# Two attention stages of one transformer layer pair on Trainium2: where a turned tile is rounded and its rest made in the second of them

## What is computed

```python
def moba_attention(q, k, v, rp_table):          # q, k, v: [B, T, H, dh], H = 8, dh = 64
    scale = dh ** -0.5
    ...
    s_own = jnp.einsum('hqd,hld->hql', qi, k_own) * scale + table_t[:, rel_bucket(d_own)]
    s_own = jnp.where(d_own[None] >= 0, s_own, -jnp.inf)
    ...
    p = jax.nn.softmax(s, axis=-1)
    return jnp.einsum('hqcl,hqcld->hqd', p_sel, v_sel) + jnp.einsum('hql,hld->hqd', p_own, v_own)

def second_block(x, mem, ...):
    h = rms_norm_2(x, norm_mix[l])
    qa, ka, va, qg, kg, vg, glr, rg = jnp.split(h @ w_in[l], offsets, axis=-1)
    o_a = moba_attention(qa, ka, va, rp_table)
    o_g = gla_chunked(qg, kg, vg, log_a)
    o_g = rms_norm_2(o_g, g_norm[l]) * jax.nn.silu(rg)
    x = x + jnp.concatenate([o_a, o_g], axis=-1) @ w_out[l]
    ...
```

## Time and profile before

| What | us |
|---|---|
| median of 3 runs | 1201.62 (1201.52 to 1201.82) |
| profiled execution | 1203.21, its span 1201.3 |
| busy: PE / DVE / ACT / POOL | 1185.0 / 741.9 / 622.9 / 146.2 |
| moba, 595 to 673 us: busy PE / DVE / ACT | 75.90 / 59.29 / 51.68 |
| fox, 60 to 140 us: busy PE / DVE / ACT | 80.00 / 49.79 / 48.54 |

### The profile page before, as it was taken

How to read it: one execution, slowest core, us unless ns; L and a number is a source line. 1 busy time by engine, 2 the same in 40 slices (tenths; PEclk the granted TensorE clock), 3 DMA queues, 4 the chain that set the end, 5 groups by cost and what they waited for, 6 DMA issues and landing times.

```text
span 1201.3 us, 16154 instructions
## 1 busy us (share of the span) xinstructions
PE 1185.0 (99%) x6066; PEld 988.1 (82%) x6066; DVE 741.9 (62%) x1124; ACT 622.9 (52%) x1054; POOL 146.2 (12%) x236
## 2 busy tenths in 40 slices
PE   9999999999999999999999999999999999999997
PEld 7788888678888888888788898888898888888886
DVE  6666567765333465674377775355647658559478
ACT  5556685675232345632676555352456355454464
POOL 3023123410000020000133100010001010000010
PEclk9999999999999999999999999999999999999999
DMA  6422234113443434342112445221286463753732
GB/s 197 106 53 54 71 105 106 36 53 105 105 105 105 158 112 137 105 127 71 50 54 105 158 125 160 85 88 53 89 245 140 149 150 88 217 116 87 211 71 88
DMA packets 151883, 133.35 MB, mean 111 GB/s; under 512 B 5313, under 2 KB 124161, under 8 KB 151810
## 3 DMA queue, kind: packets, MB, share of 16 engines
q1 hardware_dynamic: 144688, 113.13, 31.4%
q0 software_dynamic: 3744, 13.63, 5.9%
q10 hardware_dynamic: 3378, 5.60, 1.4%
HBM read 115.55 MB, written 4.22 MB: 100 GB/s over the span
## 4 chain that ended last, share of the span: by engine, by line
PE 93%; DVE 4%; ACT 2%; issue 1%; POOL 0%; DVEq 0%; ACTq 0%; POOLq 0%
PE lin L958 24%; PE lin L960 23%; PE lin L959 23%; PE tr L1140 2%; PE sc L960 2%; PE sc L959 2%; PE sc L958 2%; PE sc L1150 1%; PE sc L1152 1%; PE tr L958 1%; PE tr L960 1%; PE tr L959 1%; PE tr L1133 1%; PE lin L1176 1%; PE lin L1175 1%; DVE neg_max L2360 1%
## 5 line engine op out<-in xcount | busy, mean ns | idle before, releaser
L958 PE MATMUL lin<-h_hi,w_hi 128*128 128x512 f32 (+1 forms) x824 | 317.5, 385 | 0.0
L960 PE MATMUL lin<-h_hi,w_lo 128*128 128x512 f32 (+1 forms) x824 | 309.9, 376 | 0.0
L959 PE MATMUL lin<-h_lo,w_hi 128*128 128x512 f32 (+1 forms) x824 | 309.7, 376 | 0.0
L2335 DVE TENSOR_TENSOR w_lo<-w_raw,w_hi 128x1024 fp32r<-128x1024 f32 x160 | 195.9, 1228 | 139.0 <-ACT w_hi L1601 138.1
L1601 ACT ACTIVATE w_hi<-w_raw 128x1024 fp32r<-128x1024 f32 x162 | 170.7, 1055 | 143.1 <-PE lin L960 48.6
L960 PEld LDWEIGHTS lin<-h_hi,w_lo 128*128 128x128 f32 x824 | 155.4, 189 | 28.6
L958 PEld LDWEIGHTS lin<-h_hi,w_hi 128*128 128x128 f32 x824 | 155.7, 189 | 27.4 <-issue 0.7
L959 PEld LDWEIGHTS lin<-h_lo,w_hi 128*128 128x128 f32 x824 | 155.9, 189 | 24.7
L2360 DVE TENSOR_REDUCE neg_max<-sc 128x1 f32<-128x128 f32 (+3 forms) x112 | 52.5, 478 | 51.1 <-PE sc L1152 31.1
L2335 DVE TENSOR_TENSOR u_lo<-u_raw,u_hi 128x256 fp32r<-128x256 f32 (+2 forms) x48 | 37.4, 779 | 71.3 <-ACT u_hi L2219 38.7
L1639 ACT ACTIVATE p<-sc,neg_max 128x128 f32<-128x128 f32 (+1 forms) x80 | 42.2, 527 | 66.6 <-DVE neg_max L2360 66.1
(11 more groups left out here) (397 smaller groups left out, 2355.3 us busy)
## 6 DMA issues: line engine op xcount, KB each, us to landing
w_raw<-in_w_in SPq DMA_DIRECT2D x74, 512.0 KB, 3.9
w_raw<-in_w_up SPq DMA_DIRECT2D x32, 512.0 KB, 4.3
wd_b<-in_w_down SPq DMA_DIRECT2D x24, 512.0 KB, 5.2
w_raw<-in_w_out SPq DMA_DIRECT2D x16, 512.0 KB, 3.5
w_raw<-in_w_xkv SPq DMA_DIRECT2D x16, 512.0 KB, 4.0
x_m<-in_x SPq DMA_DIRECT2D x8, 512.0 KB, 6.1
w_raw<-in_w_branch SPq DMA_DIRECT2D x8, 512.0 KB, 4.0
w_raw<-in_w_xq SPq DMA_DIRECT2D x8, 512.0 KB, 4.0
```

Source lines behind the costliest of these rows:

```text
L958: pe.matmul(o, lh, rh, start=start, stop=False)
L959: pe.matmul(o, lh, rl, start=False, stop=False)
L960: return pe.matmul(o, ll, rh, start=False, stop=stop)
L2335: return dve.tensor_tensor(out, x, as_f32(hi), ALU.subtract)
```

## The change

The moba stage is called with `soon=True` on ACT and DVE. The work that was tied to `exps`, `maxima` and `inverses` is tied to the rounding and to the rest instead: the roots and `next_hi("va2", 3)` behind a rounding, in the steps in which they were; ACT's `split_y` one step sooner; the norms, gates, `next_lo("va2", 3)` and DVE's `split_y` behind a rest, in the steps in which they were. PE, POOL and SP have the same queues as before.

```diff
@@ ACT
             def moba_hi(m):
+                probs_hi(R0["moba"] + m, m, G["moba_pv"])
                 if m + 4 in ROOTS_BEFORE:
                     head_roots(1, lambda h: B["g_d"][:, h // 2, h % 2, :], (ROOTS_BEFORE.index(m + 4),))
-                probs_hi(R0["moba"] + m, m, G["moba_pv"])
-
-            def moba_exps(m):
-                causal_exps("moba", R0["moba"])(m)
-                if m == 5:
+                if m == 2:
                     next_hi("va2", 3)
-                if 17 <= m < 21:
-                    split_y(8 + m - 17, 4 + m - 17)
+                if 13 <= m < 17:
+                    split_y(8 + m - 13, 4 + m - 13)
...
-            attention("moba", 32, moba_hi, moba_exps, moba_out,
+            attention("moba", 32, moba_hi, causal_exps("moba", R0["moba"]), moba_out,
                       moba_fill, lambda end: 2 if end < 20 else 1, moba_first,
-                      (moba_split(0), moba_split(1)))
+                      (moba_split(0), moba_split(1)), soon=True)
@@ DVE
-            def moba_max(m):
-                causal_max("moba")(m)
-                if m - 1 in ROOTS_BEFORE:
-                    head_norms(1, B["y_1"], roots, (ROOTS_BEFORE.index(m - 1),))
-                if m - 3 in ROOTS_BEFORE:
-                    gla_gate(ROOTS_BEFORE.index(m - 3))
-                if m == 6:
+            def moba_lo(m):
+                probs_lo(R0["moba"] + m, m)
+                if m + 2 in ROOTS_BEFORE:
+                    head_norms(1, B["y_1"], roots, (ROOTS_BEFORE.index(m + 2),))
+                if m in ROOTS_BEFORE:
+                    gla_gate(ROOTS_BEFORE.index(m))
+                if m == 3:
                     next_lo("va2", 3)
-
-            def moba_invert(m):
-                invert(S0["moba"] + m)
-                if 17 <= m < 21:
-                    split_y(8 + m - 17, 4 + m - 17)
+                if 14 <= m < 18:
+                    split_y(8 + m - 14, 4 + m - 14)
...
-            attention("moba", 32, moba_max, lambda m: probs_lo(R0["moba"] + m, m), moba_invert,
+            attention("moba", 32, causal_max("moba"), moba_lo, lambda m: invert(S0["moba"] + m),
                       moba_out, moba_fill, lambda end: 3 if end < 26 else 2 if end < 28 else 1,
-                      (moba_split(0), moba_split(1), moba_split(2)))
+                      (moba_split(0), moba_split(1), moba_split(2)), soon=True)
```

## The result

The changed kernel takes **1212.31 us** (1211.05 to 1212.99), before 1201.62 (1201.52 to 1201.82): a ratio of 1.0079, with an interval of 1.0064 to 1.0095. The direction was as forecast. The time lies above the forecast of 1207.9 and above the range's end of 1211.0. The profiled execution took 1211.05 with a span of 1209.1, where before's has 1201.3: 7.8 us more, where the steps of the prediction gave 6.3.

The account below looks back on a forecast made before the run. The prediction took TensorE (PE), busy 1185.0 of 1201.3 us, to bound the kernel. PE 6.4 us later at tile 24, less a last wait of about 0.1, gave +6.3 and a median of 1207.9 us, range 1203.2 to 1211.0.

Parts of the forecast that it names:

- maximum of tile 5 to that of 19: Fourteen moba steps on DVE: 28.1 us as in fox plus moba's additions, 41.3 us in all.
- norms and gates in it: Four norms (2.4 us) and four gates (2.8 us) behind DVE's rests lengthen the moba steps.
- scores of tile 21 later than before: On PE in moba, these scores wait for the exponentials of tile 19 and start 5.0 us later.
- scores of tile 24 later than before: On PE in moba, these scores wait for POOL's key doubling behind tile 21 and start 6.4 us later.
- whole stage: Moba as a whole costs PE 6.3 us: 6.4 at tile 24 less before's last wait, about 0.1.
- DVE's waits for `pt_hi`: In moba, DVE waits for ACT's rounding some 20 times, 15 to 20 us, and seldom for scores.
- PE's waits: In moba, PE waits at scores for ACT's exponentials, first near step 9; all its waits there come to 9 us.
- after the stage: Behind moba, PE goes on without a pause in which the 6.3 us could hide.
- The loop and its price: In moba, maximum, exponentials, rounding and rest run one after the other, lengthened by work behind the rests: +6.3 us.
- The rival of the clock: TensorE's clock also falls in moba's new waits, losing 1.7 us more, for 1209.6 us; chance 7%.
- worse than fox shows: Rival in moba: late loads behind late splits and late ACT cost 3 us more, 1211 and up; chance 6%.

Follow-up runs that it names:

- a1_after: The changed kernel run again with no edit, beside the kernel before on the same chip: 1209.62 us, ratio 1.0063.
- c2_no_gates: The changed kernel without the four norms and four gates on DVE in moba: 1204.72 us, ratio 1.0022.
- c3_dve_only: Only DVE's half of the change, ACT as before, against the kernel before: 1226.57 us, ratio 1.0199.

## Why the prediction was right and where it failed

| Step | Forecast | Shown |
|---|---|---|
| maximum of tile 5 to that of 19 | 41.3 | 41.37 (a1_after) |
| norms and gates in it | 5.2 | 4.84 (c2_no_gates) |
| scores of tile 21 later than before | 5.0 | 5.2 |
| scores of tile 24 later than before | 6.4 | 6.6 |
| whole stage | 6.3 | 6.2 |
| DVE's waits for `pt_hi` | 20 times, 15 to 20 us | 23 times, 19.4 us |
| PE's waits | 9 us, at scores first near step 9 | 6.3 us, at scores first in step 11 |
| clock falls in moba | 7%; nothing in the sum | in 1 of 3 traces; 7 of 12 runs under .997 |
| after the stage | no pause | 0 to 1.4 us more |

The mechanism of the forecast was right and its +6.3 us for moba too. The step that failed is what it set around that sum: TensorE's clock at nothing, and PE going on behind the stage without a pause.

**The loop and its price were right.** Maximum, exponentials, rounding and rest as fox has them, with the extras of moba added where the order puts them, gave the time of fourteen steps to 0.1 us, and each link to PE to 0.2. That the fourteen steps agree to 0.1 us is partly luck: norms and gates were 0.4 too high in it, so something else was as much too low. With the clock in full, the one such run took 1207.77, and a1_after's span is 1205.9 where before's profiled one, less the 1.7 of its own fall near 468 us, is 1199.6: 6.3. The forecast that PE's waits come to 9 was too high: a part of the loss stands with the weight loads, which wait 10.2 us in 14 waits where before they waited 3.9 in 9.

**The rival of the clock was mispriced, in its chance and in its number.** I gave it 7% and one fall, because PE would still be busy over 80% and "in moba, with its present waits, it is 1.00 throughout". In the 32 us ahead of the fall (600 to 632 us in the first trace) PE was busy for 27.4, 86%, so the estimate of the busy share was right and the conclusion from it wrong. And before's clock was no evidence for the change: the wait at tile 16, 2.10 us with 0.58 behind it, is three times the longest in before's moba (0.7, rows 2). The price of a fall was near in size, 1.3 us in moba for 1.7.

**The forecast was for an execution without the fall near 468 us, and gave it no chance.** The rows came from an execution of before that had this fall; its median came from three whose times, 1201.52 to 1201.82, are those of runs without it (their clocks are not on record). Adding 6.3 to that median is right for a like execution of the change, but it takes the full clock ahead of moba as given. In 23 of before's 63 runs the mean clock is .997 and the time 1.7 higher. The change's first trace has this fall and the one in moba; its two other runs, at .995, are lower in the clock still and have no trace.

**"After the stage PE goes on without a pause" failed.** I looked for what would hide the loss there, and not for what would add to it. In the three traces of the change that part is 0.3 longer, the same, and 1.4 longer.

Together: 1201.6 + 6.2 for the loop, 1.7 for the fall near 468, 1.3 for one in moba and 0.3 after the stage are 1211.1; the profiled execution took 1211.05. The median, 1212.31, is another execution, without a trace, and its further 1.3 us are open; a second fall in moba or a longer last part would each be of that size. The range ended at 1211.0 since the clock and "worse than fox shows" came in only as rivals of 3 us at most, one at a time, where the first trace has two falls and a longer end in one execution.

## What to carry to other kernels

When an operation is moved closer to what it waits for, follow the semaphores round: if the path comes back to the engine on which it stands, its queue is closed to a loop, and what stands in the queue between the end of the wait and the loop's next link is paid almost in full (4.84 of 5.2 us here). One tile of distance opened it again and gave back 7.2 us: move the producer sooner and leave the consumer where it was. A new wait on TensorE can have a second price, the clock behind it: here a fall cost 1.3 us more in an execution that had it. A forecast should give it a chance and room in the range, and times should be compared between executions with the same falls.

## What the chip showed that I had not expected

- TensorE's clock is not the same in two executions of one kernel, on data and instructions that don't change. Near 468 us it falls in some and not in others, in both cases behind 0.14 us of idle time in 450 to 460 us and none in 460 to 468; before's time differs by 1.7 us of 1202. A difference of 0.14% between two single executions can be this alone.
- A wait of 2.1 us inside a stretch in which PE is busy for 84 to 86% was followed by the lower level in one trace of the same queue of PE (0.43 for 0.23 a matmul) and by the full clock in three others. In c3_dve_only a wait of 1.33 us had the lower level behind it, in a1_after one of 1.15 us had not. 13 of the 22 runs of kernels with a wait of 2.1 us have a mean clock under .997, and 3 of 135 of the others.
- 14 more matmuls on PE, in its waits, cost nothing: 69.33 and 69.37 us from scores 5 to 31, without them 69.33.
